# ScalarE's two convolution tanh moved behind a weight split, PE's four parts without a loop, and a pooling product without its zero blocks

## What is computed

```python
def pool_mixer(u, pool_w, pool_scale):          # windows 2, 4, 8, 16
    ...
        lo = jnp.maximum(t + 1 - w, 0)
        win_sum = cs[:, 1:, sl] - cs[:, lo, sl]
        d = win_sum / cnt[None, :, None] - uf[:, :, sl]
        outs.append(d @ pool_w[gi].astype(f32))

def ssd_mixer(...):
    xbc = jax.nn.silu(causal_depthwise_conv(xbc, conv_w, conv_b)).astype(f32)
```

## Time and profile before

| what | value |
|---|---|
| device time, median of 3 runs | 2273.07 us (2271.69 to 2273.22) |
| profiled execution, first to last instruction | 2272.0 us |
| PE busy in it | 2222.8 us, 98% |
| VectorE, ScalarE busy | 1159.8 us, 692.0 us |
| the four parts | about 131.6 us each, from 146 us to about 665 us |

### The profile page before, as it was taken

One profiled execution on the slowest core, in us unless ns is written; L12 is line 12 of the kernel. 1 busy time (PEld: TensorE's weight loads), 2 busy tenths in 40 slices (PEclk: granted clock), 3 DMA queues, 4 the chain that ended last, 5 costly groups with the idle time before them and its releaser, 6 DMA issues.

```text
span 2272.0 us, 32579 instructions
## 1 busy us (share of the span) xinstructions
PE 2222.8 (98%) x12776; PEld 1608.6 (71%) x12776; DVE 1159.8 (51%) x1461; ACT 692.0 (30%) x761; POOL 13.0 (1%) x28
## 2 busy tenths in 40 slices
PE   8999999999999999999999999999999999999996
PEld 8999999999988888888887954444444444444442
DVE  5356666666665554555456734444444443344335
ACT  4333433434344334334334411111111111111112
POOL 1000000000000000000000000000000000000000
PEclk9999999999999999999999999999999999999998
DMA  7444434444445555555658289999999999999996
GB/s 282 139 168 141 166 130 149 158 149 141 149 166 190 199 185 197 191 187 194 228 193 299 109 375 428 426 428 428 429 428 429 429 429 428 428 428 429 428 428 279
DMA packets 62183, 635.45 MB, mean 280 GB/s; under 512 B 7424, under 2 KB 7552, under 8 KB 10384
## 3 DMA queue, kind: packets, MB, share of 16 engines
q1 hardware_dynamic: 60192, 627.30, 70.3%
q0 software_dynamic: 752, 4.75, 0.6%
q10 hardware_dynamic: 1152, 2.10, 0.2%
HBM read 632.02 MB, written 2.10 MB: 279 GB/s over the span
## 4 chain that ended last, share of the span: by engine, by line
PE 73%; DMA 18%; DVE 5%; ACT 2%; issue 2%; SPq 0%; DVEq 0%; ACTq 0%
PE bank L304 25%; PE bank L272 19%; DMA wgu<-wgu 16%; PE bank L852 13%; PE bank L900 5%; PE bank L527 3%; PE bank L800 3%; PE bank L810 3%; DVE wlo L1222 1%; DMA raw<-units 1%; ACT whi L948 1%; DVE wlo L1559 1%; DVE cv L1337 1%; DMA wdt_raw<-wdt 1%; PE bank L833 0%
## 5 line engine op out<-in xcount | busy, mean ns | idle before, releaser
L1222 DVE TENSOR_TENSOR wlo<-raw,whi 128x2048 fp32r<-128x2048 f32 x185 | 424.0, 2292 | 397.9 <-ACT whi L948 395.8
L948 ACT ACTIVATE whi<-raw 128x2048 fp32r<-128x2048 f32 x185 | 353.9, 1913 | 430.1 <-PE bank L304 320.0
L852 PE MATMUL bank<-wgu,xg 128*64 128x512 f32 x2048 | 448.8, 593 | 4.1 <-DMA wgu<-wgu 4.1
L852 PEld LDWEIGHTS bank<-wgu,xg 128*64 128x64 f32 x2048 | 145.6, 137 | 300.4 <-issue 281.9
L272 PE MATMUL bank<-xhi,whi 128*128 128x256 f32 x896 | 260.5, 291 | 3.9 <-DVE wlo L1222 3.9
L272 PE MATMUL bank<-xhi,wlo 128*128 128x256 f32 x896 | 253.4, 283 | 0.0
L272 PE MATMUL bank<-xlo,whi 128*128 128x256 f32 x896 | 253.4, 283 | 0.0
L900 PE MATMUL bank<-wd,eactT 128*64 128x512 f32 x1024 | 226.8, 595 | 0.0
L304 PE MATMUL bank<-whi,xhi 128*128 128x512 f32 x512 | 199.8, 390 | 0.0
L1739 DVE SCALAR_TENSOR_TENSOR eact<-eth,bank 128x256 f32<-128x256 f32 x32 | 13.5, 422 | 364.7 <-issue 192.7
L304 PE MATMUL bank<-whi,xlo 128*128 128x512 f32 x512 | 199.2, 389 | 0.0
(11 more groups left out here) (364 smaller groups left out, 3409.3 us busy)
## 6 DMA issues: line engine op xcount, KB each, us to landing
wgu<-wgu SPq DMA_DIRECT2D x128, 2048.0 KB, 21.6
raw<-units SPq DMA_DIRECT2D x204, 1024.0 KB, 5.0
wd<-wd SPq DMA_DIRECT2D x64, 2048.0 KB, 18.7
raw<-units SPq DMA_DIRECT2D x6, 512.0 KB, 6.9
stage<-units SPq DMA_DIRECT2D x2, 1024.0 KB, 12.9
h<-xtok POOLq DMA_DIRECT2D x2, 1024.0 KB, 8.6
out<-acc SPq DMA_DIRECT2D x3, 512.0 KB, 2.6
stage<-units SPq DMA_DIRECT2D x2, 512.0 KB, 9.2
```

The source lines that it names most:

```text
L852: mi = nc.tensor.matmul(bank[3][CAP * j:CAP * j + CAP, :], buf[:, 4 * c + k, CAP * (2 * half + j):CAP * (2 * half + j + 1)], wgu_t[c][:, j ...
L948: nc.scalar.activation(whi[u % SPLIT][:, :], raw[u % RAW][:, :], ACT.Copy).then_inc(hi_done, 1)
L1222: V.tensor_tensor(wlo[u % SPLIT][:, :], raw[u % RAW][:, :], whi[u % SPLIT][:, :].bitcast(f32), ALU.subtract).then_inc(lo_done, 1)
```

## The change

There are three edits. On ScalarE the tanh of convolution outputs 0 and 1, with the copy of the attention result that stood behind it, moves from u = 12 to u = 13, so it comes behind split 13; the tanh of outputs 2 and 3 moves from u = 14 to u = 15, behind split 15. On PE the loop over three parts is a Python loop now, so all four parts are written out. And of the pooling matrix, PE multiplies the first block of source tokens by 144 result columns and the second by 128, where it was 256 and 256; the columns left out are zero for windows of up to 16.

```diff
+BAND = 16
...
             for c in range(2):
-                for t in range(TT):
-                    m = mm(bank[3][:, c * S:(c + 1) * S], upool[:, t, c * P:(c + 1) * P], poolmix[:, t, :],
-                           t == 0, t == TT - 1)
+
+                for t, cols in enumerate((slice(0, P + BAND), slice(P, S))):
+                    m = mm(bank[3][:, c * S + cols.start:c * S + cols.stop], upool[:, t, c * P:(c + 1) * P],
+                           poolmix[:, t, cols], t == 0, t == TT - 1, skip_group_check=True)
...
-        with pe.Fori(0, PARTS - 1) as p:
-            part(p, False)
-        part(PARTS - 1, True)
+        for p in range(PARTS):
+            part(p, p == PARTS - 1)
...
                 if u == 12:
                     act.wait_ge(unit_used, half_count(p, 6))
                     nc.scalar.activation(up[:, 2:4, 3:3 + S], b3(2), ACT.Copy).then_inc(s["up_ok"], 1)
+                if u == 13:
                     act.wait_ge(s["cv_ok"], cnt(p, 2, 1) + START)
                     act.wait_ge(s["yss_ps"], p + START)
                     nc.scalar.activation(tc[:, 0:2, :], cv[:, 0:2, :], ACT.Tanh, scale=0.5).then_inc(s["tc_ok"], 1)
...
                     nc.scalar.activation(th[:, :, :], b3(0), ACT.Tanh, scale=0.5).then_inc(s["gt_ok"], 1)
+                if u == 15:
                     act.wait_ge(s["cv_ok"], cnt(p, 2, 2) + START)
                     nc.scalar.activation(tc[:, 2:4, :], cv[:, 2:4, :], ACT.Tanh, scale=0.5).then_inc(s["tc_ok"], 1)
```

## The result

The changed kernel took 2257.22 us (median of 4 runs, 2255.07 to 2259.19), the kernel before 2273.14. The ratio is 0.9933 with a 95% interval of 0.9922 to 0.9945: 15.9 us less, where 14.1 were forecast, and inside the range of 2256 to 2265. Measured again in a later group it took 2259.48 us, a ratio of 0.9941 (0.9928 to 0.9955).

What follows compares the result with a forecast made beforehand. PE was taken to bound the kernel, with feeders late at single places. Savings of 10.5 + 3.2 + 0.3 = 14.0 us took the profiled 2272.0 to 2258.0; with 1.07 for the median, 2259.0 us, range 2256.0 to 2265.0.

Steps and rivals of the forecast that it cites:

- Edit 1: ScalarE's tanh moved behind splits 13 and 15: PE's eight waits for VectorE's `lo` go, 10.5 us over four parts.
- the refill of 0.25 us: PE at splits 13 and 15: a gap also breaks matmul overlap, so each saving is 0.25 us above the printed gap.
- What is late next: PE's `half(7, 0)` on split 14: VectorE's `lo` still ends in time, with a new margin of 0.2 us.
- the rival that the wait comes back there: Before split 14: VectorE 0.5 us later than counted costs PE 2.2 us, or 4.4 with split 15; 2261 to 2263.5, chance 0.17.
- Edit 2: PE's pooling product with fewer columns: eight records in 0.93 us instead of 1.72, saving 3.2 us in all.
- Edit 3: PE's parts written out instead of looped: gain at the first two edges 0.3 us, against 1.8 by the gaps.
- what PE no longer loses at the edge it loses in front of split 22: At the first two edges, the gaps of 0.95 and 0.85 us give way to a 0.78 us wait for `lo`.
- the chain to split 22: PE's last sums of squares, ScalarE's square root, split 21, its `lo`, VectorE's 3.36 us reciprocal; claimed as long as before.
- The sum: Whole kernel: 10.5 + 3.2 + 0.3 = 14.0 us saved.
- All of it arrives: After the parts: later work starts by PE's progress and the expert stream begins earlier by the same time, so 14.0 us arrive.

Runs made afterwards that it cites:

- the added steps: Changed kernel with the first step of conv(2) on VectorE made three times instead of once; 2261.42 us, ratio 0.9951 to the kernel before.
- the square roots moved: Changed kernel with ScalarE's two square roots moved behind split 21 and PE's loop over three parts put back; 2256.63 us, ratio 0.9931 to the kernel before.

## Why the prediction was right, point by point

**Edit 1** was said to be worth 10.5 us; alone it moved the stretch by 11.03, of which about 0.4 are what was left of narrower gaps at the edges. That the refill of 0.25 us counts beside each printed gap was the term that had to be right: the printed gaps alone give 8.5.

**What is late next**: split 14, with a margin of 0.2 us. The place was right and no wait came, but the margin was mis-sized. The prediction counted from the end of the `lo` to PE's start, which measured 0.22 as forecast, and left out the 0.14 us that PE takes between them even when it waits. By the added steps the margin was 0.07 us, so the rival that the wait comes back there was nearer than its sum says: a tenth of a microsecond of VectorE work in each part would have begun it. Its price was too high in turn: half a microsecond of lateness would cost 0.5 - 0.07 = 0.43 us a part, 1.7 in all by this estimate and not 2.2, since the refill is part of the lateness.

**Edit 2** was said to be worth 3.2 us and gave 3.20. The price followed the columns, 0.94 us for eight records where the proportion said 0.93.

**Edit 3** was said to be worth 0.3 us, against 1.8 by the gaps alone. It gave 0.28 alone, and in company with edit 1 nothing, since the gaps were narrower there. The step "what PE no longer loses at the edge it loses in front of split 22" is shown by two runs: with the parts written out alone the wait of 0.78 us stands there, and with the chain to split 22 shortened the loop costs 1.80 us.

**The sum** of 14.0 met 14.06 in the stretch. The forecast for the whole, 2259.0, lies above the first median of 2257.22 and within half a microsecond of the second, 2259.48. What it did not have is the spread of the stage before the parts, 3.4 us in the profiles, which comes from the clock.

**All of it arrives**: from the merge to the end the profiles of before and after take 1606.2 and 1605.0 us, the expert stage is as long as before (924.2 and 924.4 us from its first matmul to its last), and no load kept its absolute time.

## What to carry to other kernels

Two engines that feed each other in program order should do what the third engine waits for before they wait for each other: here a split of 1.9 us, moved ahead of a wait twice in each of four parts, was worth 10.5 us and more. A printed gap on PE is less than its price, by 0.25 us here, and a gap that a later wait covers is worth next to nothing until that wait is gone (here 0.28 us of 1.8); a place where the code already has the new form (here the last part) shows this in the profile of before. Judge a small change by a stretch that repeats, not by the whole time, if some other stage has a spread of its own.

## What the hardware showed that I had not expected

The granted clock of TensorE fell to one half inside a row of 64 matmuls of 32 and 16 columns, though PE was busy without a gap by its records. It stayed low for 6.8 or 13.7 us in different executions of the same program, and fell twice for about 3.4 us behind rows of 22. With one pair of them behind three large ones it did not fall. The Trainium skill ("TensorE: Matmul & The Clock Gate", "What's actually happening") says that the gate follows how busy the array has been; these runs agree in that the same 64 matmuls brought the clock down in a row and not when spread out. They show that PE's busy share in the profile does not tell it, and they leave open how it counts a small matmul. This dip also seems to be much of the run-to-run spread: 2270.67 to 2274.40 us for the kernel before in that group, 0.18 us without the dip; four runs are few, so that much is an observation. The mean granted clocks agree with it: in the group of the changed kernel's second measurement, the kernel before took 2271.13 to 2272.07 us in the executions with 0.995 and 2272.13 to 2274.10 in those with 0.994. It is not the only dip. In five of the twelve profiles the clock was at one half once more, for 3.4 us near 1280 to 1290 us; in the changed kernel's second profile it is there (granted 0.57 from 1284 to 1288 us), in its first it is not.

The idle at the edge of PE's loop had no fixed size: 0.95 and 0.85 us before, 1.01 and 0.59 with only the pooling edit, 0.45 and 0.35 with only the tanh moved, 0.67 and 0.61 with the square roots moved. The runs don't say what sets it.
